# Band attention scores as two fp32r products over the whole array instead of one fp32 product on a 64-row tile

## The reference, cut to what matters

```python
scores = jnp.einsum('bnqhgd,bnkhd->bnhgqk', q, k_band).astype(jnp.float32) * (dh ** -0.5)
logits = jnp.where(mask[None, :, None, None], scores + bias[None, None], jnp.float32(-1e30))
p = jax.nn.softmax(jnp.concatenate([logits, sink_l], axis=-1), axis=-1)[..., :-1]
out = jnp.einsum('bnhgqk,bnkhd->bnqhgd', p.astype(v_band.dtype), v_band)
```

## Time and profile before

| | |
|---|---|
| median of 3 runs | 2994.46 us (2993.77 to 2999.53) |
| profiled execution, first to last instruction | 2994.8 us (no other time of it is listed) |
| band attention, first score product to the last copy of its result | 103.75 to 379.60 us |
| TensorE busy, whole span | 2862.1 us (96%) |
| VectorE, ScalarE, GpSimd busy | 1866.5 (62%), 1297.7 (43%), 578.4 us (19%) |
| mean granted TensorE clock | 0.983 of full speed |

### The profile page before, as it was taken

One profiled execution on the slowest core, in us unless ns is written; L12 is line 12 of the kernel. 1 busy time (PEld: TensorE's weight loads), 2 busy tenths in 40 slices (PEclk: granted clock), 3 DMA queues, 4 the chain that ended last, 5 costly groups with the idle time before them and its releaser, 6 DMA issues. The chain is left out here.

```text
span 2994.8 us, 37617 instructions
## 1 busy us (share of the span) xinstructions
PE 2862.1 (96%) x14023; PEld 2269.2 (76%) x14023; DVE 1866.5 (62%) x2932; ACT 1297.7 (43%) x2039; POOL 578.4 (19%) x377
## 2 busy tenths in 40 slices
PE   7999998999999999899999999999999998999999
PEld 4766675778887777577898888777878776888886
DVE  6455687778877478746555022644352337999997
ACT  4355634642223242434444211222221226899995
POOL 1000020000002455210000221221122111544443
PEclk9999999999999999999999999999999998999999
DMA  6000063664445756413012222100222225778774
GB/s 249 29 22 15 8 246 148 199 220 160 163 147 205 282 182 249 166 54 119 24 31 78 70 71 78 56 28 28 91 72 70 100 107 189 259 268 273 256 262 169
DMA packets 116407, 407.32 MB, mean 136 GB/s; under 512 B 23556, under 2 KB 29988, under 8 KB 104736
## 3 DMA queue, kind: packets, MB, share of 16 engines
q1 hardware_dynamic: 82104, 348.82, 32.3%
q10 hardware_dynamic: 16440, 39.98, 3.7%
q0 software_dynamic: 17712, 16.52, 2.5%
HBM read 402.05 MB, written 82.66 MB: 162 GB/s over the span
## 5 line engine op out<-in xcount | busy, mean ns | idle before, releaser
L646 PE MATMUL psum<-ff_g,ffo_w_split 128*128 128x512 f32 x1056 | 253.3, 400 | 17.6 <-POOL ffo_w_split L566 11.1
L566 POOL TENSOR_TENSOR ffo_w_split<-ffo_w_raw,ffo_w_split 128x352 fp32r<-128x352 f32 x120 | 135.7, 1162 | 610.2 <-ACT ffo_w_split L511 610.2
L646 PEld LDWEIGHTS psum<-ff_g,ffo_w_split 128*128 128x128 f32 x1056 | 201.1, 192 | 64.9 <-POOL ffo_w_split L566 14.8
L4122 DVE TENSOR_TENSOR ex_g_lo<-ex_g_raw,ex_g_hi 128x1024 fp32r<-128x1024 f32 x188 | 220.9, 1216 | 1.2 <-ACT ex_g_hi L4059 1.1
L1027 PE MATMUL psum<-fi_t_sum_hi,fi_w_sum 128*128 128x512 f32 x704 | 220.2, 389 | 0.0
L4059 ACT CAST ex_g_hi<-ex_g_raw 128x1024 fp32r<-128x1024 f32 x188 | 191.9, 1053 | 1.9 <-PE psum L4002 1.9
L1027 PEld LDWEIGHTS psum<-fi_t_sum_hi,fi_w_sum 128*128 128x128 f32 x704 | 132.1, 188 | 27.4
L4000 PE MATMUL psum<-ex_g_hi,ex_x_hi 128*128 128x512 f32 x376 | 151.0, 402 | 0.0
L4002 PE MATMUL psum<-ex_g_hi,ex_x_lo 128*128 128x512 f32 x376 | 147.1, 391 | 0.0
L4001 PE MATMUL psum<-ex_g_lo,ex_x_hi 128*128 128x512 f32 x376 | 147.1, 391 | 0.0
L1027 PE MATMUL psum<-fi_t_sum_lo,fi_w_sum 128*128 128x512 f32 x352 | 136.9, 389 | 0.0
(11 more groups left out here) (645 smaller groups left out, 7677.6 us busy)
## 6 DMA issues: line engine op xcount, KB each, us to landing
ex_g_raw<-in_w_experts_gu_dram SPq DMA_DIRECT2D x32, 2048.0 KB, 8.8
ex_d_raw<-in_w_experts_d_dram SPq DMA_DIRECT2D x32, 1024.0 KB, 9.0
fi_raw<-in_ffn_in_dram SPq DMA_DIRECT2D x22, 1024.0 KB, 5.4
ffo_w_raw<-in_ffn_out_dram SPq DMA_DIRECT2D x31, 704.0 KB, 6.7
wom_w<-in_mod_w_dram SPq DMA_DIRECT2D x8, 2048.0 KB, 8.3
fi_first_raw<-in_ffn_in_dram SPq DMA_DIRECT2D x22, 512.0 KB, 4.6
ff_g<-fi_g SPq DMA_DIRECT2D x43, 256.0 KB, 2.0
ml_raw<-in_w_ml_dram SPq DMA_DIRECT2D x16, 512.0 KB, 4.4
```

What stands on the lines that cost most here:

```text
L566: last = nc.gpsimd.tensor_tensor(w_lo[:, v % 2, cols], w_raw[:, v % 2, cols], w_hi[:, v % 2, cols].bitcast(F32), ALU.subtract)
L646: mm = nc.tensor.matmul(chip.psum[:, 2 * u + h, :], w[:, v % 2, k * P:(k + 1) * P], (a[u] if isinstance(a, tuple) else a)[:, c * n_kc + k, ...
L4122: nc.vector.tensor_tensor(cols(g_lo, n), cols(raw.g_raw[i % 3], n), cols(g_hi, n).bitcast(F32), ALU.subtract).then_inc(q["g_lo_made"], 1)
```

## The change

The queries of a head no longer lie in 64 partitions beside those of the other head. Each head of a pair gets a tile of its own with 128 partitions: in one half lie its 64 rows rounded to fp32r, in the other half what the rounding left over. For head 0 the rounded part is in partitions 0 to 63, for head 1 in 64 to 127. The key tile, which holds the 64 key rows twice, is split into a rounded tile and a remainder tile of 128 partitions each. The scores of a head are then two products over all 128 rows, one with the rounded keys and one with the remainder, added up in PSUM. That makes four matmuls for a pair.

The copy out of PSUM becomes two steps. `round_out` on ScalarE writes the rounded part: one copy of 128x1024 for a key tile, two copies of 64x1024 for a query tile. `rest_out` on VectorE takes `copy_out`'s place and subtracts: one operation of 128x1024 for a key tile, two of 64x1024 for a query tile, each written to the other half of the partitions. `rest_out` waits for `round_out` (new semaphore `qk_rounded`), and `qk_ready` counts two for a tile where it counted one. Nothing is added to or taken from DMA or GpSimd; the new tiles use SBUF space that is free in this phase.

```diff
-    q = chip.place("ba_q", [P, 2, S], F32, B_AT)
-    key = chip.place("ba_k", [P, 2, S], F32, B_AT + 8 * KIB)
+    q = [[chip.place(f"ba_q{m}{i}", [P, S], F32R, at) for i, at in enumerate(places)]
+         for m, places in enumerate(((B_AT, B_AT + 4 * KIB), (W_AT + 4 * KIB, W_AT + 12 * KIB)))]
+    key = [[chip.place(f"ba_k{u}{part}", [P, S], F32R, at + 4 * part * KIB) for part in range(2)]
+           for u, at in enumerate((B_AT + 56 * KIB, B_AT + 8 * KIB))]
...
         @block.scalar
+            def round_out(s):
+                g, part = divmod(s, 3)
+                act.wait_ge(projected, s + 1)
+                b = bank_of(s)
+                src = chip.psum[:, b:b + 2, :].rearrange("p h t -> p (h t)")
+                if part == 1:
+                    nc.scalar.copy(key[g % 2][0][:], src).then_inc(qk_rounded, 2)
+                else:
+                    for i, rows in enumerate((slice(0, DH), slice(DH, P))):
+                        nc.scalar.copy(q[part // 2][i][rows, :], src[rows, :]).then_inc(qk_rounded, 1)
+
+            round_out(0)
             split_hi(2)
+            round_out(1)
             for j in range(NP + 6):
...
+                for s in range(2, TILES):
+                    if j == ready_before[s]:
+                        round_out(s)
...
         @block.vector
-            def copy_out(s):
+            def rest_out(s):
                 g, part = divmod(s, 3)
-                dve.wait_ge(projected, s + 1)
                 b = bank_of(s)
-                to = (q[:, 0, :], key[:, g % 2, :], q[:, 1, :])[part]
-                nc.vector.tensor_copy(to, chip.psum[:, b:b + 2, :].rearrange("p h t -> p (h t)")).then_inc(qk_ready, 1)
+                src = chip.psum[:, b:b + 2, :].rearrange("p h t -> p (h t)")
+                if part == 1:
+                    hi, lo = key[g % 2]
+                    dve.wait_ge(qk_rounded, 2 * s + 2)
+                    nc.vector.tensor_tensor(lo[:], src, hi[:].bitcast(F32), ALU.subtract).then_inc(qk_ready, 2)
+                else:
+                    for i, (rows, other) in enumerate(((slice(0, DH), slice(DH, P)), (slice(DH, P), slice(0, DH)))):
+                        both = q[part // 2][i]
+                        dve.wait_ge(qk_rounded, 2 * s + i + 1)
+                        nc.vector.tensor_tensor(both[other, :], src[rows, :], both[rows, :].bitcast(F32), ALU.subtract).then_inc(qk_ready, 1)
...
         @block.tensor
             def project(s, a, b):
-                        pe.wait_ge(qk_ready, 1 if s == 2 else s)
+                        pe.wait_ge(qk_ready, 2 if s == 2 else 2 * s)
...
             def scores(j):
-                pe.wait_ge(qk_ready, 3 * g + 2 + m)
+                pe.wait_ge(qk_ready, 2 * (3 * g + 2 + m))
                 if j >= 1:
                     pe.wait_ge(logits, 2 * j)
                 for i in range(2):
-                    rows = slice(i * DH, (i + 1) * DH)
-                    nc.tensor.matmul(chip.psum[:, i, 0:nk * P], q[rows, m, n * P:(n + 1) * P],
-                                     key[rows, g % 2, b0 * P:(b0 + nk) * P], start=True, stop=True).then_inc(scored, 1)
+                    for part in range(2):
+                        mm = nc.tensor.matmul(chip.psum[:, i, 0:nk * P], q[m][i][:, n * P:(n + 1) * P],
+                                              key[g % 2][part][:, b0 * P:(b0 + nk) * P], start=(part == 0), stop=(part == 1))
+                    mm.then_inc(scored, 1)
```

More of the change, by code:

```diff
@@ L2043, in band_attention @@
     pr = [five[:, u, :] for u in range(5)] + [sixth[:]]
+    qk_rounded = chip.sem("ba_qk_rounded")
     (sink_in, sunk, cleared, projected, qk_ready,
@@ L2165, in normalise @@
                     nc.vector.tensor_scalar(part, part, stats[:, RD, at + i:at + i + 1], None, ALU.mult).then_inc(normed, 1)
-            copy_out(0)
+            rest_out(0)
             weights.split_lo(dve, nc.vector, 2)
-            copy_out(1)
+            rest_out(1)
             dve.wait_ge(sink_in, 16)
@@ L2184, in _ @@
                     if j == ready_before[s]:
-                        copy_out(s)
+                        rest_out(s)
         @block.tensor
```

## The result

The changed kernel takes 3006.15 us (median of 7 runs, 3000.23 to 3010.48) against 2993.77 for the kernel before in the same job (7 runs, 2992.32 to 2999.53): a ratio of 1.0036, with a 95% interval of 1.0026 to 1.0047. A second job gave 1.0035 (1.0022 to 1.0048). The change makes the kernel 0.36% slower, about 11 us. The forecast was 2995.5 and no measurable change; the result lies above its range.

A forecast was written before the change was run, and what follows sets the result against it. TensorE was taken to bound units with a projection share, a chain through three engines the tail. Terms -12.2 + 8.0 + 3.15 + 1.05 + 1.0 = +1.0 us on the 2994.8 span, less 0.3 for the median: 2995.5, range 2990 to 3003.

The forecast's parts named there:

- units behind a share: Units whose scores come straight after a projection share: 42 not following a tile end save 0.29 us each, 12.2 us.
- six query tiles: Ends of tiles 2, 3, 5, 6, 8, 9: next projection share waits for rounding and subtraction, 8.0 us lost.
- three key tiles: Ends of tiles 4, 7, 10: the chain before the scores grows by one rounding and handover, 1.05 us each, 3.15 together.
- tile 1: Its end stands directly before the first scores: 1.05 us lost.
- tile 11 and tail: After the last projection: VectorE's chain starts 2.2 us later, new scores give back 1.2; net 1.0 us lost.
- rival (C): Slower: new products' weight loads stand open, about 3011 us, 2%; second half, granted clock falls in TensorE's new pauses, another 2%.
- Unit savings: TensorE time per unit: 0.10 us into the scores, 0.14 in the score block, 0.05 at the transposes; 0.29 in all.
- Rival (E): Score products: heads lose their side-by-side run for nothing, 52 units lose 0.7 us each, about 3043 us; 1%.
- Pauses behind tile ends: Six TensorE pauses before projection shares: 1.8 us after tiles 3, 6, 9 and 1.3 after 2, 5, 8, nine together.
- Rival (B): Slower at query tiles: ScalarE and VectorE don't overlap, or half-tile operations cost more; +6.6 us, about 3002; 13%.
- (D): Faster: 64-row operations take half the time, so the 8.0 us of query tile ends vanish, about 2987 us; 9%.

The follow-up runs named there:

- `fill`: The changed kernel plus 176 extra TensorE matmuls of 128x256 into unused PSUM, filling the pauses at tile ends: 2995.12 us, ratio 1.0005 to the kernel before.
- `again`: The changed kernel timed and profiled once more, nothing edited: 3005.21 us, ratio 1.0035 to the kernel before.
- `scores_only`: The changed kernel's score products, but VectorE copies the tile out at once as before, remainders left out: 2977.97 us, ratio 0.9947 to the kernel before.
- `ends_only`: The changed kernel's ScalarE and VectorE steps at tile ends, written into one fp32 tile, with the old score products: 3013.72 us, ratio 1.0061 to the kernel before.
- `rowtile3`: Against the kernel before: three fp32r score products per head on the 64-row tiles, one rounding and one subtraction of 128x1024 per tile end: 3002.64 us, ratio 1.0029.
- `staged_fill`: The changed kernel with six query tiles first copied whole to SBUF, and filling matmuls in the five remaining pauses: 2984.45 us, ratio 0.9965 to the kernel before.

## Why the prediction was wrong

`fill` has no fall of the clock in the band, so its unit distances show each term of the sum by itself:

| term | predicted | measured |
|---|---|---|
| units behind a share | −12.2 (42 at 0.29) | −13.3 (43 at 0.30, three after `apply` together −0.4) |
| six query tiles | +8.0 | +9.0 (three of 1.69 to 1.73, three of 1.24 to 1.31) |
| three key tiles | +3.15 | +3.9 (1.31 each) |
| tile 1 | +1.05 | +1.2 |
| tile 11 and tail | +1.0 | +1.8 |
| sum | +1.0 | +2.5 |
| granted clock | 0 | 0 in `fill`, +9.3 in the change, +7.7 in `again` |

**The step that failed is a term that the sum did not have: the granted clock.** The changed kernel's band is 9.3 us longer than that of `fill` and has six stretches at half speed: 1.55 each (1.54 in `again`), close to the 1.7 that half of 3.41 us would be if TensorE set the pace all through. The case was named, as the second half of rival (C), given 2%, and not priced. The reason given against it was that the clock stayed at 1.00 between 350 and 380 us with TensorE idle for a sixth of the time. The runs don't bear that inference out. The idle time of that stretch was in small pieces but for one, where TensorE waited 1.55 us for VectorE (timeline before):

```profile
365.15 0.88 PE L2223 MATMUL psum<-ident,ba_probs 128*128 128x128 f32 x6 [1.55 <-DVE ba_probs L2165]
```

One such pause without a fall, and one of 1.89 at the first matmul of the output product, say little when six falls come behind eleven pauses of 1.5 to 2.9 us. The eleven pauses were all in the working; what wasn't asked is what TensorE's clock does after them.

**Unit savings: right.** 0.23 into the scores, a block of 0.70 (0.71 forecast), 0.30 in a unit. Four fp32r products over the whole array take 0.70, three fp32r pairs side by side 0.73 and the fp32 pair 0.85. Rival (E) is out. The page "TensorEngine Tiling (Array Packing)" of the Trainium skill, section "Theoretical Speedup", promises up to 2x from row tiling. These numbers show that the change lost nothing by giving it up; the 2x itself, the same products on a 64-row tile with and without a neighbour, is measured in no run here.

**Pauses behind tile ends: right in place and count, mis-sized by 0.2 for a query tile.** 1.97 and 1.54 against 1.8 and 1.3. The forecast took the overlap of whole-tile operations from the earlier trace rows for half-tile ones, which have none. For VectorE this agrees with what the Trainium skill says under "VectorE: DVE Perf Modes", "Two Vector instructions with no wait between them": an instruction whose input or output starts on another quarter of the partitions than that of the one ahead is held until that has ended. The text gave some 1 us for it and left it out of the sum; measured, the six query tiles cost 1.0 more. That ScalarE behaves likewise, 1.03 apart with lengths of 1.007, was in no row. Rival (B) is out in its form (ScalarE and VectorE do overlap: the first subtraction starts at 147.72, the second rounding has started at 147.71), and so is (D): a half-tile operation costs as much as a whole one, 1.007 against 1.012 on ScalarE and 1.22 against 1.22 on VectorE.

**Key tiles: mis-sized.** 1.31 and not 1.05 for each. In `scores_only`, without the extra rounding and handover, the same three distances already grew by 0.16. Counted from the last projection matmul, the scores come after 2.82 before, 2.88 in `scores_only` and 3.98 in the changed kernel. So the real cost is 1.16; 0.09 of the 1.31 are the shorter way into the scores ahead, which the first row of the table counts as a saving, and some 0.05 come from the filling matmuls, with which it is 4.03.

**Tail: mis-sized.** The unit of tile 11 and the one after it lose 2.65 (2.2 forecast), and the seven units behind give back 0.9 (1.2 forecast).

**Both halves add up only without the clock.** By medians of one job `scores_only` is 16.5 faster and `ends_only` 19.3 slower than before, together +2.8; the whole change is +10.8. In the bands of the halves there are none and three falls, in that of the whole six and five. Without falls the bands add up: −15.1 and +16.0 make +0.9, and the six units behind query tiles, which save 0.3 each in `scores_only` only, bring that to +2.7, against +2.5 in `fill`. Why the shorter units bring more falls from the same pauses stays open: single profiles can't tell it from chance. Open too is what picks the pause. In the two profiles of the changed kernel the falls in the band came behind pauses of 1.65 and more (those of 1.65 and 1.66 have a second one of 0.48 behind them) and never behind the three of 1.54. But in `ends_only` one came behind 1.34 and in `rowtile3` one behind 1.43; and at or behind the 1.89 ahead of the output product one came in `again`, `scores_only`, `ends_only` and `rowtile3`, and none in the other six profiles. No experiment varied the length of one pause alone.

## What to carry to other kernels

When a change puts a pause into an engine that was full, price it twice: its length, and what TensorE's clock does after it. Here eleven pauses of 1.5 to 2.9 us, 13 us in the plan, brought 8 to 9 us on top, and matmuls without use in those pauses brought them back. And free the PSUM bank with one plain copy: here two engines in a row on a bank that the next matmul waits for cost 10.7 us more on six tiles than one further copy of each and rounding and subtraction that nobody waits for (`fill` against `staged_fill`).

## What the runs showed of the hardware that was not expected

- The granted clock fell from 2.4 to 1.2 GHz for 3.41 us (once 6.83) at or up to 2.2 us behind pauses of TensorE of 1.3 to 2.9 us; six and five times behind the eleven pauses in two executions of one kernel, not at the same ones, and not in the band of the two kernels in which all these pauses were filled.
- Of two operations on 64 partitions each, one half after the other, the second starts when the first has ended: 1.03 apart on ScalarE (length 1.007), 1.25 on VectorE (1.22). Whole-tile ones start 0.95 and 1.14 apart.
- Three pairs of fp32r matmuls on two 64-row tiles (384 columns) take 0.73 in a unit, where one fp32 pair takes 0.85 and four fp32r matmuls of the whole array 0.70.
